# Two-layer hybrid encoder on eight cores: weights in runs of 512 columns, and another order of loads, transposes and stores

## The chip, the cores and the metric

One Trainium2 chip. The kernel runs on its 8 cores; each core takes one of the 8 sequences of the batch and holds nothing of the others. The time is the device time in microseconds of the slowest core, the median of several runs. A core has five engines that run side by side, each in the order of its own instructions: TensorE (PE) for matmuls, VectorE (DVE), ScalarE (ACT), GpSimd (POOL) and SyncE (SP). DMAs are issued by SP, ACT and POOL and run on 16 DMA engines per core.

## The reference

Two layers over x of 4096 positions by 1024 channels per core, then a final norm.

```python
def even_mixer(h, w_in, conv_w, conv_b, ln_g, ln_b, pool_w, pool_scale, w_out):
    z = h @ w_in                                                    # (B, S, 1536)
    a, gate, p = z[..., :D_A], z[..., D_A:2 * D_A], z[..., 2 * D_A:]
    ya = conformer_conv(a, gate, conv_w, conv_b, ln_g, ln_b)
    yb = multiscale_pool(p, pool_w, pool_scale)
    return jnp.concatenate([ya, yb], axis=-1) @ w_out

def spatial_gating(u, v, v_ln_g, v_ln_b, spatial_w, spatial_b):
    vn = layernorm(v.reshape(bn, s, N_SGU, H_D), v_ln_g, v_ln_b)
    vn = vn.reshape(bn, s // CHUNK, CHUNK, N_SGU, H_D)
    sv = jnp.einsum('hqk,bnkhc->bnqhc', spatial_w, vn) + spatial_b.T[:, :, None]
    return u * sv.reshape(bn, s, D_D)

for l in range(DEPTH):
    h = rmsnorm(x, mix_norm_g[l])
    x = x + (even_mixer if l % 2 == 0 else odd_mixer)(h, ...)
    h = rmsnorm(x, ffn_norm_g[l])
    x = x + (silu(h @ w_gate) * (h @ w_up)) @ w_down
return rmsnorm(x, final_norm_g)
```

`conformer_conv` is a gated linear unit, a depthwise convolution of width 31, a LayerNorm over 512 channels and a silu. `multiscale_pool` averages over centred windows of 2, 4, 8 and 16 positions. `odd_mixer` projects h to c (512 channels, a 2-D Fourier transform per head), and to u and v (a gelu, then the spatial gating above in chunks of 128 positions). The FFN is 2816 wide.

## The kernel before

The 4096 positions are 32 tiles of 128. A transposed, normalised activation of all tiles lives in `BIG` (32 tiles of 8 x 128 columns, 2 bytes each); matmuls read it as weights or as moving data, 512 columns at a time. Everything is written by hand in program order: `k.op`, `k.mm` and `k.dma` (L155 to L190) put the waits in front of each instruction, and every matmul has line L171, every DMA line L185, so one tells them apart by tiles. Weights are float32 in memory and become bfloat16 on the way; only POOL issues such DMAs (queue q0 in the profile). SP issues nearly all others (q1), transposes among them. `banks` hands out six PSUM banks in turn (eight in the odd layer's mixer).

Stages, in the order of the program:

1. *Even projections.* `norm_step` (L739) moves a tile through load (`n_load`), square and root (`n_stat`), scale, and transpose (`n_tr`: on TensorE for tiles 0 to 7, by DMA from SP after that). `p_proj` (L661) makes the pooling part and stores it through `pst`; `ag` (L670) makes gate and value and the gated unit. The list `jobs` mixes them, eight `p_proj` first. `n_load` of tiles from 2 on waits for the first third of the weights (`w_in`, `load_w_in`). `late_consts` loads the constants for the convolution after `ag` 3.
2. *Pooling and convolution*, `pool_bank` and `conv`, into `z`.
3. *First output projection, even layer.* `prologue` (L879) projects tiles 0 to 7: residual add on VectorE, norm, and a DMA transpose of `hbp`. Between its steps `feed0` (L904) runs the convolution's LayerNorm by groups of tiles: `ln_stat` (VectorE, POOL), `ln_norm` (ScalarE, into a ring of four tiles `vn`, then a DMA transpose into `BIG`), `ln_silu` (ScalarE, in place).
4. *FFN.* `ffn` (L476) goes over four chunks of 8 tiles: 22 steps j of gate and up (`up`: 32 matmuls of 512 columns, a ScalarE silu into `tmp`, a VectorE product), then eight tiles of the down projection. `Weights.fetch` keeps four steps of `wgu` in flight, 0.5 MB each as bfloat16, in every chunk anew; `wd` comes in the first chunk and stays. A table `steps` hangs the output projection of the next chunk's tiles (`op.load`, `op.mm`, `op.add`, `scale`, `tr`) on the steps j. In the first chunk `bg0` (L934) hangs the rest of the LayerNorm there too: for each group (n, a), `ln_stat` at j = a, `ln_norm` at a + 1, `ln_silu` at a + 2.
5. *Odd mixer.* `c_proj` (L987) for 16 tiles, its results through four staging tiles `cst` to memory; constants; then a loop over i with `u_proj`, `v_proj`, `v_stat`, `v_rs`, `v_norm` (four ScalarE operations a tile, one on POOL) and `sv` (L1067), staggered by up to 8 tiles, with the first Fourier steps (`f_first`) in between. Its last eight rounds have no projection left: each runs one `sv`, one `f_gcs_part`, one `f_s1` and one `v_norm`.
6. *Rest of the Fourier transform, prologue and FFN of the odd layer*, the same code as 3 and 4 without the LayerNorm, and the final norm.

`sv` adds the bias inside the matmul: for each of four heads a product with 128 rows, and one with 2 rows that carries the bias:

```python
mms.append((ps[:, b, h * 128:(h + 1) * 128], vn[:, t % 3, h * 128:(h + 1) * 128], swT[:, h, :], True, False))
mms.append((ps[:, b, h * 128:(h + 1) * 128], blT[0:2, h * 128:(h + 1) * 128],
            sbrow[0:2, h * 128:(h + 1) * 128], False, True))
```

## Time and profile before

| | |
|---|---|
| median of 3 runs | 2738.52 us (2737.62 to 2747.39) |
| profiled execution, own time | 2747.14 us |
| its span, slowest core (core 3) | 2746.0 us |
| spans of the 8 cores | 2727.0 to 2746.0 us |
| TensorE busy | 2584.3 us, 94% of the span, 12795 matmuls |
| VectorE, ScalarE, POOL busy | 812.7, 657.7, 331.6 us |
| chain that ended last | TensorE 84%, DMA 5%, SP's queue 4%, ScalarE 2%, issue 2% |
| DMA | 339.8 MB landed, HBM read 331.89 MB and written 83.89 MB |

A busy TensorE is one with matmuls in its pipeline; what counts beside it is the granted clock (1.00 is 2.4 GHz, 0.50 is 1.2 GHz) and the number of matmuls in a stretch. A wait is put down to the instruction that came last; idle time of an engine other than the one that sets the pace costs nothing by itself.

### The profile page before, as it was taken

What the parts mean: (1) busy time and instruction counts of PE and PEld (TensorE: products, weight loads), DVE (VectorE), ACT (ScalarE), POOL (GpSimd) and SP (SyncE); (2) the same over time, 40 slices, a digit from 0 to 9 for tenths busy, and PEclk for the clock granted to TensorE, in tenths of its full rate; (3) what the DMA queues carried; (4) which work ended last, traced back from release to release, by engine and by line L of the source; (5) the groups of instructions that cost most, each with busy time, mean ns of one, the idle gap of its engine ahead of it and who ended that gap; (6) DMA issues with size and microseconds to landing.
All of it is one profiled execution on the core that took longest, in us unless ns stands there. A gap on an engine that the chain in (4) does not pass through costs nothing.

```text
span 2746.0 us, 38570 instructions; the slowest of 8 cores (2727.0 to 2746.0 us)
## 1 busy us (share of the span) xinstructions
PE 2584.3 (94%) x12795; PEld 1210.6 (44%) x12795; DVE 812.7 (30%) x1175; ACT 657.7 (24%) x1163; POOL 331.6 (12%) x644
## 2 busy tenths in 40 slices
PE   5899786699999999999998998999999999999998
PEld 2346332344444444444443446444444444444443
DVE  2334532222222222222222445422222222222212
ACT  2333532311111121111113565211111111111111
POOL 1210111110100011000010341111011001100000
PEclk7999898899999999999999998999999999999999
DMA  6886689963665489444463104988356536554422
GB/s 150 189 174 141 154 134 127 131 144 125 126 126 137 126 158 154 139 102 77 111 152 92 70 9 98 205 165 169 93 123 132 115 108 127 124 119 108 77 45 95
DMA packets 257790, 339.80 MB, mean 124 GB/s; under 512 B 172350, under 2 KB 185152, under 8 KB 256448
## 3 DMA queue, kind: packets, MB, share of 16 engines
q1 hardware_dynamic: 222080, 218.68, 30.4%
q0 software_dynamic: 35376, 118.38, 26.5%
q8 instruction: 112, 1.84, 0.3%
q14 instruction: 78, 0.64, 0.1%
q10 hardware_dynamic: 144, 0.26, 0.0%
HBM read 331.89 MB, written 83.89 MB: 151 GB/s over the span
## 4 chain that ended last, share of the span: by engine, by line
PE 84%; DMA 5%; SPq 4%; ACT 2%; issue 2%; DVE 1%; POOL 1%; ACTq 0%; DVEq 0%; POOLq 0%
PE ps L171 84%; SPq L185 4%; DMA BIG_43<-vn_3454 2%; DMA xin_51<-x 1%; ACT BIG_43 L833 1%; DMA w_in_56<-ev_w_in 1%; ACT vt_12677 L1060 0%; DVE hb_91 L384 0%; POOL vn_12679 L1064 0%; DMA wd_3963<-ffn_wd 0%; DMA cdr<-cst_12665 0%; POOL rs_12682 L1046 0%; ACT vn_3454 L824 0%; ACT hb_91 L378 0%; DVE bst_2166 L804 0%
## 5 line engine op out<-in xcount | busy, mean ns | idle before, releaser
L171 PE MATMUL ps<-BIG_43,wgu_3455 128*128 128x512 bf16 x2816 | 621.4, 382 | 56.9 <-ACT tmp_3965 L495 43.6
L171 PE MATMUL ps<-BIG_43,wgu_16581 128*128 128x512 bf16 x2816 | 612.4, 379 | 0.0
L171 PEld LDWEIGHTS ps<-BIG_43,wgu_3455 128*128 128x128 bf16 x2816 | 276.8, 98 | 397.1 <-issue 71.1
L171 PEld LDWEIGHTS ps<-BIG_43,wgu_16581 128*128 128x128 bf16 x2816 | 275.6, 98 | 332.2
L171 PE MATMUL ps<-wd_3963,gT_3964 128*128 128x512 bf16 x1408 | 306.4, 380 | 3.8 <-DMA wd_3963<-ffn_wd 3.8
L171 PE MATMUL ps<-wd_16931,gT_16932 128*128 128x512 bf16 x1408 | 304.7, 379 | 2.6 <-DMA wd_16931<-ffn_wd 2.6
L497 DVE TENSOR_TENSOR gT_3964<-tmp_3965,ps 128x512 bf16<-128x512 f32 x176 | 120.9, 687 | 470.8 <-PE ps L171 361.8
L497 DVE TENSOR_TENSOR gT_16932<-tmp_16933,ps 128x512 bf16<-128x512 f32 x176 | 121.1, 688 | 419.6 <-PE ps L171 408.7
L171 PEld LDWEIGHTS ps<-wd_3963,gT_3964 128*128 128x128 bf16 x1408 | 138.2, 98 | 171.4 <-issue 6.5
L171 PEld LDWEIGHTS ps<-wd_16931,gT_16932 128*128 128x128 bf16 x1408 | 137.7, 98 | 168.9 <-issue 3.1
L495 ACT ACTIVATE tmp_16933<-ps 128x512 f32<-128x512 f32 x176 | 104.6, 594 | 395.4 <-PE ps L171 383.1
L495 ACT ACTIVATE tmp_3965<-ps 128x512 f32<-128x512 f32 x176 | 104.4, 593 | 365.6 <-PE ps L171 333.0
L171 PE MATMUL ps<-w_in_56,BIG_43 128*128 128x512 bf16 x768 | 178.5, 397 | 12.3 <-ACT sg_100 L679 7.9
L378 ACT ACTIVATE hb_3457<-xr_3456 128x1024 bf16<-128x1024 f32 x56 | 59.2, 1056 | 433.0 <-DVE xr_3456 L520 287.5
L361 POOL TENSOR_TENSOR ssb_44<-ssb_44,epsd_49 128x1 f32<-128x1 f32 x159 | 29.8, 188 | 1093.1 <-ACT hb_3457 L378 453.2
L171 PE MATMUL ps<-w_out_2713,BIG_43 128*128 128x512 bf16 x512 | 118.8, 387 | 16.7 <-ACT BIG_43 L833 16.3
L171 PEld LDWEIGHTS ps<-w_in_56,BIG_43 128*128 128x128 bf16 x768 | 77.6, 102 | 111.2 <-issue 28.6
L171 PE MATMUL ps<-w_in_12096,BIG_43 128*128 128x512 bf16 x512 | 115.5, 379 | 4.5 <-DVE cst_12665 L411 3.8
L171 PE MATMUL ps<-w_out_15705,BIG_43 128*128 128x512 bf16 x512 | 114.6, 379 | 1.1 <-ACT BIG_43 L409 1.1
L185 POOL DMA_DIRECT2D wgu_16581<-ffn_wgu x88 | 48.0, 546 | 482.5 <-PE ps L171 440.9
L185 POOL DMA_DIRECT2D wgu_3455<-ffn_wgu x88 | 48.5, 552 | 450.0 <-PE ps L171 449.6
L529 ACT ACTIVATE hb_16583<-xr_16582 128x1024 bf16<-128x1024 f32 x31 | 32.8, 1057 | 276.3 <-DVE xr_16582 L520 276.3
(150 smaller groups left out, 1749.5 us busy)
## 6 DMA issues: line engine op xcount, KB each, us to landing
wgu_3455<-ffn_wgu POOLq DMA_DIRECT2D x88, 512.0 KB, 6.0
wgu_16581<-ffn_wgu POOLq DMA_DIRECT2D x88, 512.0 KB, 5.4
xin_51<-x SPq DMA_DIRECT2D x32, 512.0 KB, 4.7
xr_3456<-xres SPq DMA_DIRECT2D x32, 512.0 KB, 3.9
xnat<-xr_3456 SPq DMA_DIRECT2D x32, 512.0 KB, 3.0
xr_16582<-xr SPq DMA_DIRECT2D x32, 512.0 KB, 5.5
out<-xr_16582 SPq DMA_DIRECT2D x31, 512.0 KB, 3.6
xr_3456<-x SPq DMA_DIRECT2D x28, 512.0 KB, 5.7
```

What stands on the lines that cost most here:

```text
L171: ins = self.nc.tensor.matmul(o, lhsT=l, rhs=r, start=st, stop=sp)
L185: ins = q.e.dma_start(out=o, in_=i, transpose=True) if transpose else q.e.dma_start(out=o, in_=i)
L361: k.op(pool, lambda e: e.tensor_tensor(out=ss, in0=ss, in1=epsd[:], op=ALU.add), reads=[d, d_epsd], writes=[d])
L378: k.op(act, lambda e: e.activation(out=h, in_=ap, func=AF.Square, accum_out=ssb[:, s, :]), reads=[dep], writes=[d_h, d_ss[s]])
L495: k.op(act, lambda e: e.activation(out=tmp[:], in_=ps[:, bl[0], :], func=AF.Silu), reads=[psd[bl[0]]], writes=[d_tmp])
L497: k.op(dve, lambda e: e.tensor_tensor(out=gT[:, j, tg * 512:(tg + 1) * 512], in0=tmp[:], in1=ps[:, bl[1], :], op=ALU.mult), reads=[d_tmp, ...
L529: k.op(act, lambda e: e.activation(out=h, in_=x, func=AF.Square, accum_out=ssb[:, s, :]), reads=[d], writes=[d_h, d_ss[s]])
L833: k.op(act, lambda e: e.activation(out=BIG[:, t0:t1, c, :], in_=BIG[:, t0:t1, c, :], func=AF.Silu, scale=evec[:, 0, c:c + 1], bias=evec[:, ...
```

## The change

It does nine things.

- All large weights and constants lie in memory as blocks of 128 rows by 512 columns, so that each row of a DMA is several runs of 512 elements (2 KB read, 1 KB landed) instead of one of 1024 to 4096. `dma_runs` and the layout in the host code.
- Start: x tiles 1 to 7 are issued at once, tiles 4 to 7 into a buffer of their own (`xin2`); the constants of the convolution come in three parts (after `ag` 5, 9 and 12).
- Stores of the pooling and of the c projection (`pst`, `cst`) go to ScalarE's queue; the c evacuations are all on ScalarE.
- The pooling tiles are loaded four to a DMA.
- LayerNorm groups are smaller at first; groups 0 to 4 (tiles 0 to 9) are transposed on TensorE, and the silu reads PSUM. The others keep the DMA transpose; their silu comes at j = a + 5 with new a's.
- FFN steps: the residual load two steps before its tile's base step, the projection one step after it; in the first chunk the tiles are two steps apart.
- The gating bias is one matmul of 8 rows by 512 columns, made with a selector (`sel8`, `sb8`), ahead of the four of 128 columns; `vn` has six tiles.
- The odd layer's constants are loaded during `c_proj` and used at i = 4 (`od_setup`); the Fourier constants (`gcs`) are loaded at i = 12 and 14.
- The gating loop ends with its 32nd round; the last tiles follow in a tail of their own, with the root per tile (`v_rs1`).

```diff
+        def dma_runs(q, o, i, **kw):
+            return k.dma(q, [(o.rearrange("p (b n) -> p b n", n=512), i.rearrange("b p n -> p b n"))], **kw)
...
-                    k.dma(pool, [(self.w[:, s], T["ffn_wgu"][self.l, self.n % NJ])], writes=[self.d[s]])
+                    dma_runs(pool, self.w[:, s].rearrange("p a b c -> p (a b c)"), T["ffn_wgu"][self.l, self.n % NJ],
+                             writes=[self.d[s]])
...
-                        s = (5 * n) // 2
+                        s = 3 + 2 * n if c == 0 else 1 + (5 * n) // 2
                         t = 8 * (c + 1) + n
-                        for q, fn in enumerate((op.load, op.mm, op.add, op.nrm.scale, op.nrm.tr)):
-                            steps.setdefault(s + (0, 1, 1, 2, 2)[q], []).append((fn, t))
+                        for pr, (j, fn) in enumerate(((s + 2, op.nrm.scale), (s + 2, op.nrm.tr), (max(0, s - 2), op.load),
+                                                      (s + 1, op.mm), (s + 1, op.add))):
+                            steps.setdefault(j, []).append((pr, n, fn, t))
...
-        k.dma(sp, [(xin[:, 1, :], T["x"][1])], writes=[d_xin[1]])
+        for t in range(1, 8):
+            n_load(t)
...
-            k.dma(sp, [(by_phase(pdr)[t // 16, t % 16], pst[:, r, :])], reads=[d_pst[r]], addw=[d_pdr[t // 16]],
+            k.dma(act, [(by_phase(pdr)[t // 16, t % 16], pst[:, r, :])], reads=[d_pst[r]], addw=[d_pdr[t // 16]],
...
-        groups = [(0, 2), (2, 4), (4, 8), (8, 12), (12, 16), (16, 20), (20, 24), (24, 28), (28, 32)]
+        groups = [(0, 2), (2, 4), (4, 6), (6, 8), (8, 10), (10, 13), (13, 16), (16, 20), (20, 24), (24, 28), (28, 32)]
...
         def ln_silu(n):
             t0, t1 = groups[n]
+            if n < LN_PE:
+                b = k.banks(2)
+                for t in range(t0, t1):
+                    v, d_v = lnv[t]
+                    k.mm([(ps[:, b + t - t0, c * 128:(c + 1) * 128], v[:, c * 128:(c + 1) * 128], ident[:], True, True)
+                          for c in range(4)], reads=[d_v, d_ident], writes=[psd[b + t - t0]])
+                for c in range(4):
+                    k.op(act, lambda e: e.activation(out=BIG[:, t0:t1, c, :], in_=ps[:, b:b + 2, c * 128:(c + 1) * 128],
...
-            for n, a in ((4, 1), (5, 3), (6, 6), (7, 9), (8, 12)):
+            for n, a in ((5, 0), (6, 2), (7, 4), (8, 7), (9, 10), (10, 13)):
                 if j == a:
                     ln_stat(n)
                 if j == a + 1:
                     ln_norm(n)
-                if j == a + 2:
+                if j == a + 5:
                     ln_silu(n)
...
-            evac(t % 2, cst[:, t % 4, :], ps[:, b, :], [psd[b]], [d_cst[t % 4]])
-            k.dma(sp, [(cdr[t * 128:(t + 1) * 128, :], cst[:, t % 4, :])], reads=[d_cst[t % 4]], addw=[d_cdr],
+            evac(0, cst[:, t % 4, :], ps[:, b, :], [psd[b]], [d_cst[t % 4]])
+            k.dma(act, [(cdr[t * 128:(t + 1) * 128, :], cst[:, t % 4, :])], reads=[d_cst[t % 4]], addw=[d_cdr],
...
-            mms = []
+            mms = [(ps[:, b, :], blT[0:8, :], sbrow[0:8, :], True, False)]
             for h in range(4):
-                mms.append((ps[:, b, h * 128:(h + 1) * 128], vn[:, t % 3, h * 128:(h + 1) * 128], swT[:, h, :], True,
-                            False))
-                mms.append((ps[:, b, h * 128:(h + 1) * 128], blT[0:2, h * 128:(h + 1) * 128],
-                            sbrow[0:2, h * 128:(h + 1) * 128], False, True))
+                mms.append((ps[:, b, h * 128:(h + 1) * 128], vn[:, t % 6, h * 128:(h + 1) * 128], swT[:, h, :], False,
+                            h == 3))
...
-        for i in range(NT + 8):
+        for i in range(NT):
...
+        v_stat(NT - 1)
+        v_rs1(NT - 1)
+        v_norm(NT - 6)
+        for n in range(4):
+            sv(NT - 8 + n)
+            v_norm(NT - 5 + n)
+            f_gcs_part(0, 4 * n)
+        v_norm(NT - 1)
+        for n in range(4):
+            f_gcs_part(0, 16 + 4 * n)
+            f_s1(1, range(8 * n, 8 * n + 8, 4))
+        for n in range(4):
+            sv(NT - 4 + n)
```

How the order of instructions moves, at three places. First SP, from the start of the program; `xin` and `xin_7` are x tiles, `hb` a normalised tile, `pdr` the pooling store. Before:

```order
L185 DMA xin_51<-x 128x1024
L185 DMA gbc_61<-norm_g 128x1024
L185 DMA xin_51<-x 128x1024 x2
L185 DMA pdr<-pst_99 128x512
L185 DMA xin_51<-x 128x1024
```

Now:

```order
L185 DMA xin_51<-x 128x1024
L185 DMA gbc_62<-norm_g 128x1024
L185 DMA xin_51<-x 128x1024 x3
L185 DMA xin_7_52<-x 128x1024 x4
L185 DMA xin_51<-x 128x1024 x2
L185 DMA_TRANSPOSE BIG_43<-hb_98 128x8x128
```

Ten x tiles stand ahead of the first transpose, and no store between them. Next ScalarE in the first steps of the even layer's first FFN chunk; `tmp` is the FFN silu, `vn` the LayerNorm's normalised tile, `BIG<-BIG,evec` its silu after a DMA transpose, `hb` the square of a norm. Before:

```order
L495 ACTIVATE tmp_3965<-ps 128x512
L824 ACTIVATE vn_3454<-z_29_2711,rs_2168 128x512 x4
L495 ACTIVATE tmp_3965<-ps 128x512 x2
L378 ACTIVATE hb_3457,ssb_44<-xr_3456 128x1024
L833 ACTIVATE BIG_43<-BIG_43,evec_46 128x4x128 x4
```

Now:

```order
L508 ACTIVATE tmp_3893<-ps 128x512 x5
L842 ACTIVATE vn_3355<-z_30_2633,rs_2114 128x512 x3
L508 ACTIVATE tmp_3893<-ps 128x512 x3
L842 ACTIVATE vn_3355<-z_30_2633,rs_2114 128x512 x3
L508 ACTIVATE tmp_3893<-ps 128x512 x2
L387 ACTIVATE hb_3358,ssb_44<-xr_3357 128x1024
L508 ACTIVATE tmp_3893<-ps 128x512 x2
L868 ACTIVATE BIG_43<-BIG_43,evec_46 128x3x128 x4
```

Seven FFN silus stand between the first group's normalisation and its silu, where two did. Last TensorE at the end of the gating, `gcs` and `f32m` being Fourier steps and `sbrow` the bias. Before, one of the last eight rounds:

```order
L171 MATMUL ps<-sbrow_12674,blT_12675 128x128
L171 MATMUL ps<-gcs_12667,Y_13664 128x128 x8
L171 MATMUL ps<-f32m_12673,ctm_12666 128x128 x4
L171 MATMUL ps<-swT_12670,vn_12679 128x128
L171 MATMUL ps<-sbrow_12674,blT_12675 128x128
```

Now:

```order
L171 MATMUL ps<-sbrow_12610,blT_12611 128x512
L171 MATMUL ps<-swT_12606,vn_12617 128x128 x4
L171 MATMUL ps<-gcs_12603,Y_13565 128x128 x16
L171 MATMUL ps<-f32m_12609,ctm_12602 128x128 x8
L171 MATMUL ps<-gcs_12603,Y_13565 128x128 x8
```

The Fourier steps stand together, ahead of the last four gating products.

## Rows read from the trace of the kernel before

**Rows 1.** Windows by stage: length; PE, PEld, DVE, ACT, POOL busy; PEclk, DMA share, GB/s

```profile
0.00:114.50 114.50, 75.14 (x323) 33.30 (x324) 31.19 (x29) 35.35 (x61) 20.14 (x54) 0.80 0.74 169
295.00:360.00 65.00, 42.80 (x178) 17.89 (x177) 30.88 (x48) 32.14 (x49) 12.28 (x28) 0.86 0.81 186
360.00:591.00 231.00, 179.55 (x794) 78.74 (x793) 61.62 (x103) 62.86 (x97) 36.36 (x70) 0.89 0.90 134
591.00:1410.00 819.00, 815.16 (x3770) 369.16 (x3769) 207.01 (x227) 130.67 (x226) 70.36 (x159) 1.00 0.55 125
1410.00:1451.00 41.00, 29.26 (x136) 12.60 (x134) 7.09 (x10) 5.21 (x9) 5.02 (x10) 0.96 0.94 184
1566.00:1626.00 60.00, 59.66 (x335) 31.27 (x336) 28.30 (x111) 38.09 (x76) 18.77 (x14) 1.00 0.00 1
1626.00:1668.60 42.60, 31.52 (x192) 18.79 (x193) 19.79 (x53) 23.15 (x47) 20.94 (x18) 0.61 0.21 59
1709.00:1919.00 210.00, 210.00 (x975) 95.19 (x973) 69.39 (x77) 45.03 (x77) 36.47 (x78) 1.00 0.88 179
```

**Rows 2.** Waits of TensorE, 295 to 592 us: total, times, longest

```profile
PE ps L171 <- ACT tmp_3965 L495: 43.6, 5, 20.5
PE ps L171 <- ACT BIG_43 L833: 16.3, 2, 9.1
PE ps L171 <- DVE xr_3456 L471: 7.7, 1, 7.7
```

**Rows 3.** Waits of ScalarE, 295 to 592 us

```profile
ACT BIG_43 L833 <- DMA BIG_43<-vn_3454: 66.8, 7, 23.2
```

**Rows 4.** DMA queues, 520 to 527 us: packets, MB, share of 16 engines

```profile
q0 software_dynamic: 401, 1.11, 85.4%
q1 hardware_dynamic: 509, 0.13, 27.6%
```

**Rows 5.** Chain that ended last, from the start: start us, us, what

```profile
1.65 14.18 DMA w_in_56<-ev_w_in
15.91 13.35 DMA xin_51<-x
```

**Rows 6.** Timeline of SP, 0 to 125 us: start us, us, what

```profile
40.03 0.33 SPq L185 DMA_DIRECT2D pdr<-pst_99  x1
40.51 0.33 SPq L185 DMA_DIRECT2D xin_51<-x  x1
```

**Rows 7.** Timeline of TensorE, 0 to 125 us

```profile
35.59 3.57 PE L171 MATMUL ps<-w_in_56,BIG_43 128*128 128x512 bf16 x8 [1.37 <-ACT BIG_43 L409]
...
44.94 0.61 PE L171 MATMUL ps<-ident_52,hb_91 128*128 128x128 bf16 x8
```

**Rows 8.** Groups of instructions, 284 to 345 us: busy us, mean ns; idle before

```profile
L833 ACT ACTIVATE BIG_43<-BIG_43,evec_46 128x256 bf16<-128x256 bf16 x8 | 4.8, 598 | 0.6
```

**Rows 9.** The page's DMA queues, whole run

```profile
q1 hardware_dynamic: 222080, 218.68, 30.4%
q0 software_dynamic: 35376, 118.38, 26.5%
```

**Rows 10.** DMA queues, 1415.6 to 1418 us, small constants

```profile
q0 software_dynamic: 263, 0.24, 83.3%
```

**Rows 11.** Timeline of POOL, 1385 to 1470 us

```profile
1415.30 0.56 POOL L185 DMA_DIRECT2D f32m_12673<-f32m  x1
```

**Rows 12.** Timeline of SP, 1410 to 1452 us

```profile
1422.06 10.59 SPq L185 DMA_TRANSPOSE BIG_43<-hdr  x1
```

**Rows 13.** Timeline of TensorE, 1574 to 1592 us: one tile's gating product, then Fourier

```profile
1576.20 0.22 PE L171 MATMUL ps<-swT_12670,vn_12679 128*128 128x128 bf16 x1
...
1577.47 0.62 PE L171 MATMUL ps<-f32m_12673,ctm_12666 128*128 128x128 bf16 x8
1577.93 1.89 PE L171 MATMUL ps<-w_in_12096,BIG_43 128*128 128x512 bf16 x8
```

**Rows 14.** Timeline of all engines, 1626 to 1669 us

```profile
1632.09 2.25 ACT L1060 ACTIVATE vt_12677<-vt_12677,rs_12682 128x128 f32<-128x128 f32 x4 [3.01 <-DVE rs_12682 L1052]
```

More of the change, by code:

```diff
@@ L221, with runs @@
 NAT = 16 * (np.arange(128) % 8) + np.arange(128) // 8
+def runs(a, n=512):
+    a = np.asarray(a).reshape(128, -1, n)
+    return np.ascontiguousarray(a.transpose(1, 0, 2))
 def make_consts():
@@ L242, in make_consts @@
     band = band[:, :, :, NAT]
-    c["band"] = np.ascontiguousarray(band.transpose(2, 0, 1, 3)).astype(np.float32)
+    c["band"] = runs(band.transpose(2, 0, 1, 3).astype(np.float32))
     c["ident"] = np.eye(128, dtype=np.float32)
@@ L586, in ffn @@
                     W.fetch(c * NJ + j + 1 + NSLOT)
-                    for fn, t in steps.get(j, []):
+                    for _, _, fn, t in sorted(steps.get(j, []), key=lambda x: x[:2]):
                         fn(t)
                     if c == 0:
-                        k.dma(pool, [(wd[:, j, :], T["ffn_wd"][l, j])], writes=[d_wd[j]])
+                        dma_runs(pool, wd[:, j, :], T["ffn_wd"][l, j], writes=[d_wd[j]])
                     if bg is not None:
@@ L722, in p_load @@
                 pbuf[t] = (t_[:, t - lo], d_[t - lo])
-                k.dma(sp, [(t_[:, t - lo], pdr[t])], reads=[d_pdr[t // 16]], writes=[d_[t - lo]])
+            for t in range(lo, hi, 4):
+                n = min(4, hi - t)
+                k.dma(sp, [(t_[:, t - lo:t - lo + n], pdr[t:t + n].rearrange("t p d -> p t d"))],
+                      reads=[d_pdr[t // 16], d_pdr[(t + n - 1) // 16]], writes=d_[t - lo:t - lo + n])
         jobs = [(p_proj, t) for t in range(8)]
@@ L809, in ln_stat @@
             m = t1 - t0
[L810 to L813 removed]
+            rstd(rs[:, r, 0, 0:m], mv[:, r, 0:m, 1], False, [d_mv[r]], d_rs[r])
         def ln_norm(n):
@@ L827, in ln_norm @@
                      reads=[d_z[t // 16][t % 16], d_mv[r], d_rs[r]], writes=[d_v])
-                k.dma(sp, [(BIG[:, t, 0:4, :], v)], reads=[d_v], writes=[dB[t][0]], transpose=True)
+                if n >= LN_PE:
+                    k.dma(sp, [(BIG[:, t, 0:4, :], v)], reads=[d_v], writes=[dB[t][0]], transpose=True)
+                else:
+                    lnv[t] = (v, d_v)
+        lnv = {}
+        LN_PE = 5
         def ln_silu(n):
             t0, t1 = groups[n]
+            if n < LN_PE:
[6 more added lines that the diff above has]
+                    k.op(act, lambda e: e.activation(out=BIG[:, t0:t1, c, :], in_=ps[:, b:b + 2, c * 128:(c + 1) * 128],
+                                                     func=AF.Silu, scale=evec[:, 0, c:c + 1], bias=evec[:, 1, c:c + 1]),
+                         reads=[d_evec, psd[b], psd[b + 1]], addw=[dB[t][0] for t in range(t0, t1)])
+                return
             for c in range(4):
@@ L905, in feed0 @@
             if i == -2:
-                ln_stat(0)
-                ln_norm(0)
-                ln_stat(1)
-                ln_norm(1)
+                for n in range(2):
+                    ln_stat(n)
+                    ln_norm(n)
+            if i == -1:
                 ln_silu(0)
-                ln_stat(2)
-                ln_norm(2)
-                ln_silu(1)
             if i == 0:
                 Wf.fetch(NSLOT)
-            if i == 1:
-                ln_silu(2)
-            if i == 5:
-                ln_stat(3)
-            if i == 6:
-                ln_norm(3)
-            if i == 8:
-                ln_silu(3)
-        prologue(op, 3, 2, feed0)
+            if i in (1, 3, 5):
+                ln_silu(1 + i // 2)
+                if i < 5:
+                    ln_stat(2 + i // 2)
+                    ln_norm(2 + i // 2)
+            if i == 7:
+                ln_stat(4)
+                ln_norm(4)
+            if i == 9:
+                ln_silu(4)
+        prologue(op, 2, 2, feed0)
         nrm2 = Norm(None, hbr)
@@ L1249, in prep_inputs @@
     g["od_vln"] = _rep(f(inputs["od_v_ln_g"])[0].reshape(512))
-    g["od_vln_b"] = np.stack([f(inputs["od_v_ln_b"])[0].reshape(512), np.ones(512, np.float32)])
+    vb = f(inputs["od_v_ln_b"])[0].reshape(4, 128)
+    g["od_vln_b"] = np.stack([vb, np.ones_like(vb)], axis=1).reshape(8, 128)
     sw = f(inputs["od_spatial_w"])[0]
     g["od_spatial_wT"] = np.ascontiguousarray(sw.transpose(2, 0, 1))
-    g["od_spatial_b"] = np.ascontiguousarray(f(inputs["od_spatial_b"])[0]).reshape(1, 512)
+    sb = np.zeros((4, 2, 4, 128), np.float32)
+    for h in range(4):
+        sb[h, 1, h] = f(inputs["od_spatial_b"])[0][h]
+    g["od_spatial_b"] = sb.reshape(8, 512)
     g.update(make_consts())
```

216 lines of the change are left out of this document (118 added, 98 removed).

## The prediction

> **What bounds the kernel now.** I read the stretches by stage first [rows 1]. In the long FFN stretch TensorE is busy for 815 of 819 us at full granted clock: 3770 matmuls, 0.216 us each. The reader is to look for stretches where that pace is lost. There are four. The first 114.5 us (busy 75, clock 0.80). The even layer's first output projections with the first FFN chunk, 65 + 231 us for 178 + 794 matmuls: the odd layer runs the same loop, 975 matmuls, in 210 us without a gap. The start of the odd layer (29.3 of 41). The end of the spatial gating, 42.6 us at clock 0.61. Then the waits say who ends them. Between 295 and 592 us TensorE waits 43.6 us for the FFN's ScalarE silu, 16.3 us for the LayerNorm silu and 7.7 us for a residual tile [rows 2]; but ScalarE itself waits 66.8 us, in seven pieces, for DMA transposes of the LayerNorm tiles [rows 3]. ScalarE works in order, so the FFN silu stands behind a LayerNorm silu whose tile hasn't landed. The DMA rows tell why: in seven microseconds 509 small packets of q1 (the transposes) went by 401 large ones of q0 (weights) [rows 4], about one for one, so each transpose packet sits out a weight packet.
>
> So the bound is TensorE, plus some 160 us (2746 less 2584 busy) in which it stands still. The change goes at these places; whole matmul time is nearly untouched.
>
> **The change, part by part.** A measurement of this kernel can tell about 0.5% (14 us) from no change.
>
> *Start.* Now the first weights land at 15.8 us, and x tile 2, which waits for them, at 29.3 [rows 5]; later tiles are loaded behind the store of a projection in SP's order [rows 6], so every tile pays one projection, one load and one norm in a row. At 114.5 us TensorE has done 233 of its 512-column matmuls (323 less 26 for warming and 64 transposes), 50 us at 0.216, and 64 transposes (eight in 0.61 us [rows 7], 5 us): it is 60 us behind. The change issues x 1 to 7 at once, into buffers that are free, and moves the stores to ScalarE's queue. By 29.3 us the chip had read 3 x 2.1 MB of weights, 0.5 MB of norm scale and three x tiles of 0.52 MB, 8.4 MB; the new start needs 11 MB before the last weights are there, at the same pace 38 us. Weights and x share that pace, so I put the first weights at 21 us instead of 15.8. Eight projections, each with a transpose, then cost between 2.3 us (8 x 0.216 + 0.61) and 4.2 us (3.57 + 0.61, at the clock of that stretch [rows 7]) each; I take 3.5, nearer the slow end, since TensorE has just stood idle, 28 us, to 49 us, with 14 + 5 us of that useful: 30 behind. ScalarE still meets the load of tile 12 ahead of the first sigmoid; 6 us for it. 36 instead of 60: **gain 24**, between 12 (all cold, loads as late as now) and 36.
>
> *LayerNorm of the even layer.* Tiles 0 to 9 go through TensorE: 5 pairs of 8 transposes at 0.61 us add 3 us. The silu reads PSUM in pairs: four at 0.60 us [rows 8], so three times in the prologue TensorE waits some 2.7 us, 8 us; the first chain stays at about 5, the last transposed tile of the prologue at 4, clock lost around these 3. Tiles 10 to 31 keep the DMA but the silu comes four FFN steps after the transpose instead of one, some 30 us instead of 8, and no wait for one took longer than 23.2 us [rows 3]. What is late next is the ring of four normalised tiles: ScalarE must wait for a slot before the next group; 5 us for that. Of the 86 us over the odd layer's 210, 28 stay: **gain 58**, between 30 (half of the silu waits come back through the ring) and 72. Loads of the residual three steps ahead are in it (7.7 us).
>
> *Weights in runs of 512.* A fetch of 0.52 MB becomes 512 packets of 1 KB instead of 128 of 4 KB. Price by the rows, in microseconds of one of 16 engines per MB landed: q0 over the whole run 0.265 x 16 x 2746 / 118.4 = 98 [rows 9]; a moment with small constants, 1 KB packets mostly, among other traffic 0.833 x 16 x 2.4 / 0.24 = 133 [rows 10]. I take 115, in between, since the second row is a crowded moment. The dearest place is the first FFN chunk, 22 x (0.52 + 0.26) MB = 17.3 MB: 124 us of each engine, beside 13.4 MB of other traffic (8 tiles read, written and transposed, 22 LayerNorm tiles) at q1's 61 (0.304 x 16 x 2746 / 218.7), 51 us. 175 us against the 185 us that TensorE needs: covered, narrowly. At 133 it would be 195, and 10 us in each layer show; at 98 nothing does. Cost 0; the range takes 20. The longer descriptor lists are written by POOL; nothing in the trace shows such a list. Below: no dearer than now, 0.56 us for 128 rows [rows 11]. Above: in proportion, 4.5 us for each of three weight loads ahead of tile 0's norm, 13 us, of which the weights' own landing hides most. I take 1 us each, on no path.
>
> *Odd layer's start.* TensorE is idle 41 - 29.3 = 11.7 us there [rows 1]: the four staging tiles of the c projection wait for stores that stand in SP's order behind transposes, one of which took 10.6 us to issue [rows 12]. Stores move to ScalarE's queue, with all evacuations; ScalarE is busy 5 of these 41 us and has room. **Gain 10**, between 6 and 12; constants and their 24 copies move under the u and v projections. The Trainium skill (DMA: Bandwidth & Descriptors, Issuing engines are not separate DMA queues) says that issuing from several engines saves only the issue time. By that the 16 stores would give SP some 8 us and TensorE nothing; the 10.6 us issue ahead of a store speaks for the gain, a matter of order and not of bandwidth.
>
> *Gating bias.* Eight 128-column matmuls of a tile, 128 rows and 2 rows by turns, take 1.27 us from the first's start to the end of the turns, 0.16 each, while eight like ones in a row give way after 0.46, 0.06 each [rows 13]. One of 512 columns (0.22), four at 0.06 and two changes at 0.1 make 0.65 instead of 1.27: 0.62 on each of 24 tiles where TensorE is full (59.7 of 60 us), **gain 14**, between 3 (only the number of instructions counts) and 19.
>
> *Gating tail.* The new tail has no rounds that wait one for the other. ScalarE bounds it: six normalisations at 2.25 us [rows 14], 13.5, some evacuations, 2.4, and 3 us to the last product, after 4 us of v projection: 23 instead of 42.6. **Gain 20**, between 12 and 32.
>
> The rest I put at 0: pooling tiles loaded in groups of four and the FFN steps of the later chunks lie where TensorE runs through.
>
> Sum: 24 + 58 + 10 + 14 + 20 = **126 us**. The profiled run took 2747.1, so 2621; it stands 8.6 above the median, 2738.5, and against that the forecast is **2612**.
>
> **The rivals.** *Weight packets still go out in bundles.* The Trainium skill (DMA: Bandwidth & Descriptors, Queues, rings and completion order) says that a DMA engine drains a packet of many descriptors from one ring before it turns to the next. By that rule four runs of 1 KB would pass as one 4 KB did. Worked from the rows: transposes are then as slow as now [rows 4], the ring of four tiles fills and most of the silu waits come back, in the first chunk and at the prologue's last tile: the 58 falls below its low end, to some 25. Gain 126 - 33 = 93, time 2645. For it: no row has small weight packets beside transposes. Against it: 1.27 transpose packets per weight packet, so turns are short. 0.14.
>
> *The start stays bound by reading.* x and weights share the chip's memory; if eight cores at once get less than 0.29 MB per us, x and weights land at 45 us and the gain there is about 6: 2630. 0.10. The DMA share of 0.74 [rows 1] leaves either open.
>
> *Weights come too late (slower).* In both first chunks, if 1 KB runs cost far more than 133. At 200 per MB the weights alone take 216 us of each engine, with the rest 267 against 185: 82 us lost in each layer; the other six chunks, 11.5 MB and 40 us of other traffic against 177, lose 7 each. 206 - 126 = 80 slower: 2819. It begins at 124, where the first chunks just fit (134 + 51 = 185), and turns the sign near 183 (198 + 51 - 185 = 64, twice). No row here is above 133 [rows 10]: 0.03.
>
> **How the numbers follow.** My forecast has 0.73, with 2575 to 2650 from the bounds of the terms (all low ends together 63, 2675; all high ones 171, 2567; they won't all fall on one side). The two fast rivals lie at 2645 and 2630. The range, **2575 to 2680**, leaves out the slow rival and the far ends. Faster by over 0.5% 0.96, within 0.5% 0.01, slower 0.03: even the low ends of all terms are 2.3%.
>
> **What would show it.** Right: the same waits between the prologue and the end of the first chunk add up to under 30 us, ScalarE's wait for LayerNorm transposes to under 10; that whole stretch takes some 238 us; TensorE is in its stride by 60 us; the gating tail takes about 25 us at a higher clock; q0's share rises from 26.5% to about 31%. Wrong: TensorE waits for weights in the first chunks, ScalarE waits for slots of the LayerNorm ring, or transposes still take 20 us beside weights.

## The result, and the profile after

The changed kernel takes 2674.92 us (median of 4 runs, 2664.44 to 2678.49); the kernel before, beside it, 2742.95 (4 runs). The ratio is 0.9744, interval 0.9705 to 0.9784: 68 us faster, where 126 were forecast. The profiled execution took 2678.49 us.

Spans of three cores in that execution, with the mean granted clock:

```profile
core 2: 2660.5 us, clock 0.983
core 3: 2657.3 us, clock 0.983
core 6: 2676.4 us, clock 0.979
```

Seven cores lie between 2657 and 2662; core 6 ends 15 us later and gives the time. Before, core 3 was the slowest; in the other three runs of the changed kernel cores 2, 4 and 4 were. Rows below are of core 2, a middle one, unless another is named.

The table shows by stage where the time went. Each number is the median over the 8 cores of one profiled execution, in us, between two events of the trace. The first two columns count from the start: to the first sigmoid, and to the first pooling product, where the input projections end. Then: first output projection to first FFN silu (prologue); from there to the 44th silu (chunk 1); to the 45th (its down projection); first staging tile of the c projection to VectorE's first product of u with the gate (odd start); to the last gelu of v (gating); to the first norm of the next prologue (tail). Where an edit leaves a stage alone, its entries spread over at most 4 us, in the last four columns over 2.

```
                  sigmoid  proj.end  prologue  chunk 1   down  odd start  gating   tail
before               80.6     232.5      58.8    214.2   86.2      108.2   116.2   79.6
changed              81.6     231.2      58.9    176.5   87.6       91.3   111.5   65.8
long rows            77.5     228.4      58.9    193.7   85.7       91.3   112.3   65.7
silu near            81.0     232.8      58.0    208.2   87.2       91.3   112.3   65.5
DMA transposes       81.4     232.5      67.1    174.8   87.5       90.5   113.3   66.3
early x              73.1     218.0      59.0    177.6   88.8       91.3   112.3   65.5
early x, long w_in   68.3     213.3      59.0    178.8   87.6       91.3   111.5   65.5
SP stores            78.3     226.9      59.9    176.5   87.3       91.3   111.5   66.0
table early          80.4     229.7      60.2    176.5   87.2       91.3   112.3   65.5
table early, SP st.  78.0     227.1      58.4    176.7   88.0      102.3   113.1   65.5
constants early      81.1     229.4      58.9    176.5   87.3       91.3   111.5   66.0
bias by turns        81.8     232.2      58.8    176.6   87.6       91.8   117.6   71.6
old tail             81.2     231.0      59.6    176.5   87.2       91.3   109.8   75.2
combined             69.3     213.9      49.7    178.0   81.2       91.3   111.5   65.8
```

From before to changed, chunk 1 gave 38, the odd start 17, the tail 14, gating 5, the start 1, the prologue nothing, and the down projection took 1. The sum is 73; between the two slowest cores it is 70, since core 6 stood further above the middle than core 3 had.

Windows by stage, columns as in [rows 1], of the start, the prologue and chunk 1:

```profile
0.00:60.00 60.00, 27.25 (x136) 12.47 (x137) 15.36 (x14) 19.43 (x31) 10.37 (x29) 0.77 0.74 163
293.00:352.00 59.00, 38.81 (x180) 16.99 (x178) 28.11 (x42) 28.03 (x49) 13.36 (x30) 0.87 0.74 165
352.00:529.00 177.00, 177.00 (x818) 80.11 (x817) 64.70 (x110) 67.43 (x105) 44.46 (x70) 1.00 1.15 173
```

Chunk 1 runs through at full clock now. In the start and the prologue TensorE is still idle for half and a third of the time. Its waits in the prologue, 290 to 352 us (total, times, longest):

```profile
PE ps L171 <- ACT BIG_43 L863: 7.9, 2, 5.5
PE ps L171 <- ACT vn_3355 L842: 5.0, 3, 3.4
PE ps L171 <- DVE xp_2656 L484: 4.2, 1, 4.2
PE ps L171 <- DVE hbp_3359 L393: 2.4, 1, 2.4
```

Its waits from 0 to 145 us, where norms, weights and one sigmoid hold it up:

```profile
PE ps L171 <- DVE hb_98 L393: 19.0, 5, 4.8
PE ps L171 <- DMA w_in_58<-ev_w_in: 11.8, 1, 11.8
PE ps L171 <- ACT sg_107 L699: 6.9, 2, 6.3
```

The answer to [rows 2, 3]: TensorE's waits for the FFN silu, 43.6 us on core 3, are gone from chunk 1. Of ScalarE's 66.8 us for transposes this is left in its waits from 348 to 592 us, a wait for a slot of the ring of four:

```profile
ACT vn_3355 L842 <- DMA BIG_43<-vn_3355: 6.5, 2, 4.8
```

The page's groups, which are of core 6, name what that core lost: 6.6 us for a residual tile, for which no other core waits in chunk 1, and 8.4 us for down weights, for which the others wait 3.9 to 5.8. That is some 10 of its 15 us.

```profile
L171 PE MATMUL ps<-BIG_43,wgu_3356 128*128 128x512 bf16 x2816 | 616.6, 381 | 7.0 <-DVE xr_3357 L484 6.6
...
L171 PE MATMUL ps<-wd_3891,gT_3892 128*128 128x512 bf16 x1376 | 305.3, 382 | 10.1 <-DMA wd_3891<-ffn_wd 8.4
```

The page's queues, against [rows 9]:

```profile
q0 software_dynamic: 120016, 118.40, 30.9%
q1 hardware_dynamic: 206768, 208.71, 29.3%
```

The same weights in 3.4 times as many packets cost 0.309 x 16 x 2676 / 118.4 = 112 us of an engine per MB, where 98 was the price before and 115 was assumed.

### The profile page after: what moved, and what is told of

It is laid out like the page before. It is cut to its first block, busy times and chain, and to the rows that moved or that the text cites. A ratio compares the mean times of both kernels' runs of the same rounds, so it can differ in the third digit from the quotient of the medians.

```text
span 2676.4 us, 38177 instructions; the slowest of 8 cores (2657.3 to 2676.4 us)
## 1 busy us (share of the span) xinstructions
PE 2545.3 (95%) x12585; PEld 1193.9 (45%) x12739; DVE 802.3 (30%) x1166; ACT 665.8 (25%) x1186; POOL 385.2 (14%) x655
## 4 chain that ended last, share of the span: by engine, by line
PE 86%; DMA 3%; SPq 3%; issue 2%; POOL 2%; DVE 2%; ACT 2%; another core or an unknown queue 1%; ACTq 0%; DVEq 0%; POOLq 0%
PE ps L171 86%; SPq L185 2%; DMA xin_51<-x 2%; ACT vt_12615 L1114 1%; DMA xr_3357<-x 1%; DVE hb_98 L393 1%; POOL vn_12617 L1118 0%; DMA wd_3891<-ffn_wd 0%; POOL rs_12620 L1091 0%; DMA wd_16768<-ffn_wd 0%; ACT hb_98 L387 0%; DMA gbc_62<-norm_g 0%; POOL ssb_44 L373 0%; DVE bst_2112 L825 0%
## 5 line engine op out<-in xcount | busy, mean ns | idle before, releaser
L171 PE MATMUL ps<-BIG_43,wgu_3356 128*128 128x512 bf16 x2816 | 616.6, 381 | 7.0 <-DVE xr_3357 L484 6.6
L171 PE MATMUL ps<-BIG_43,wgu_16418 128*128 128x512 bf16 x2816 | 612.4, 379 | 0.0
L171 PE MATMUL ps<-wd_3891,gT_3892 128*128 128x512 bf16 x1376 | 305.3, 382 | 10.1 <-DMA wd_3891<-ffn_wd 8.4
L171 PE MATMUL ps<-wd_16768,gT_16769 128*128 128x512 bf16 x1376 | 305.3, 382 | 6.5 <-DMA wd_16768<-ffn_wd 4.8
L171 PE MATMUL ps<-w_in_58,BIG_43 128*128 128x512 bf16 x751 | 174.7, 392 | 24.2 <-DMA w_in_58<-ev_w_in 12.2
L185 POOL DMA_DIRECT2D wgu_16418<-ffn_wgu x88 | 66.9, 760 | 470.0 <-PE ps L171 456.0
L171 PE MATMUL ps<-w_out_2635,BIG_43 128*128 128x512 bf16 x485 | 112.1, 385 | 16.0 <-ACT BIG_43 L863 8.3
L185 POOL DMA_DIRECT2D wgu_3356<-ffn_wgu x88 | 67.3, 766 | 413.9 <-PE ps L171 400.1
L171 PE MATMUL ps<-w_in_12032,BIG_43 128*128 128x512 bf16 x495 | 112.6, 379 | 2.4 <-DVE xr_3357 L533 1.5
L171 PE MATMUL ps<-w_out_15542,BIG_43 128*128 128x512 bf16 x485 | 109.1, 379 | 2.7 <-ACT BIG_43 L422 1.4
```

The source lines that it names most:

```text
L171: ins = self.nc.tensor.matmul(o, lhsT=l, rhs=r, start=st, stop=sp)
L185: ins = q.e.dma_start(out=o, in_=i, transpose=True) if transpose else q.e.dma_start(out=o, in_=i)
```

## The experiments

Twelve kernels ran. Each is the changed one with one part undone or moved; three carry two or more edits, as named. Ratios are to the kernel before. Their intervals reach some 10 us to either side, so the smaller verdicts go by the stages of the table.

### First chunk: distance, packets, transposes

**Long rows.** All weights again as one row per partition; the other shapes follow the two shown.

```diff
-    return k.dma(q, [(o.rearrange("p (b n) -> p b n", n=512), i.rearrange("b p n -> p b n"))], **kw)
+    return k.dma(q, [(o, i)], **kw)
-    "ffn_wgu": [2, NJ, 4, 128, 512],
-    "ffn_wd": [2, NJ, 2, 128, 512],
+    "ffn_wgu": [2, NJ, 128, 2048],
+    "ffn_wd": [2, NJ, 128, D],
```

> The change with the weights' long rows put back (one descriptor per partition and tile, as before), all else kept. Theory A (the silu's distance and the transposes on TensorE brought the gain of the first FFN chunk, the length of the runs does little for it): the first chunk, from the first FFN silu to the 45th, stays within 6 us of the 177 that the middle core takes with the change, and the time within 8 us of 2675. Theory B (short packets let the transposes by, and that brought the gain): the chunk is 20 us or more longer, 2690 to 2710. Theory C (short runs cost: they are behind the waits of up to 8 us for the down weights): those waits halve, the share of q0 goes from 31% back to about 27%, and the time is 5 to 12 us shorter.

Ratio 0.9784 (0.9735 to 0.9832), profiled 2697.38 us. Chunk 1 took 193.7 us, 17 more, from 186 to 216 by core: between A's 6 and B's 20, nearer B. The rows on the tile vn from 352 to 560 us say how long a LayerNorm transpose took to land. Of the changed kernel:

```profile
DMA to landing us min/median/max: 9.5/13.6/17.8
```

The same with long rows:

```profile
DMA to landing us min/median/max: 4.9/17.6/33.1
```

By core the slowest took 22 to 33 us with long rows and 15 to 20 with short ones. The distance from a normalisation to its silu is four steps (4 x 177 / 22 = 32 us). Only core 2's slowest, with long rows, is longer, and on no core does a silu wait for a landing. What comes late is the next normalisation: the ring of four is full, and ScalarE waits for a slot, 348 to 592 us, on core 2:

```profile
ACT vn L841 <- DMA BIG<-vn: 33.7, 9, 7.2
```

TensorE, in the same stretch, then waits for the FFN silu behind it:

```profile
PE ps L171 <- ACT tmp L507: 21.6, 2, 18.9
```

Theory C fell, though short runs do cost at another place: with long rows the first projection began at 19.3 us instead of 29.9.

**Silu near.** The silu of the first chunk one step behind its normalisation.

```diff
-                if j == a + 5:
+                if j == a + 2:
                     ln_silu(n)
```

> The change with the LayerNorm silu of the first FFN chunk back at one step behind its normalisation instead of four; transposes on TensorE and short runs kept. Theory A (the distance made the gain): ScalarE waits again 20 to 50 us for DMA transposes, the first chunk takes 195 to 210 us instead of 177, time 2690 to 2710. Theory B (short packets make a transpose land in time anyway): ScalarE waits under 10 us, chunk within 5 us of 177, time within 8 us of 2675.

Ratio 0.9810 (0.9749 to 0.9872), chunk 1 208.2 us, 32 more: theory A. ScalarE's wait on the core where it was longest, core 6, 348 to 592 us:

```profile
ACT BIG L868 <- DMA BIG<-vn: 51.4, 5, 16.7
```

So the distance is worth 32 us with short runs in place, the runs 17 with the distance in place, and both together with the rest 38: each covers a part of what the other does. The finer groups, their new steps and the earlier residual loads were not undone by themselves.

**DMA transposes.** No LayerNorm tile turned on TensorE.

```diff
-        LN_PE = 5
+        LN_PE = 0
```

> The change with the LayerNorm tiles 0 to 9 transposed by DMA too, the finer groups and the distance of four steps in the first chunk kept. Theory A (the transposes on TensorE serve the prologue): the prologue, 58 us with the change, takes 64 to 80, since the silu there follows its normalisation by at most one projection pair and waits for the landing, 7 us at the median and up to 15; the first chunk stays at 177. Theory B (the prologue's time is set by the chain of sums, norms and silu, and not by how the tile is turned): 58 to 61 us, since it took 59 before, with DMA transposes.

Ratio 0.9758 (0.9708 to 0.9808), prologue 67.1 us, 8 more: theory A, near its low end. TensorE's waits for the silu, 290 to 352 us:

```profile
PE ps L171 <- ACT BIG L868: 21.6, 4, 13.9
```

The transposes on TensorE save 8 us against that, and yet the prologue is no faster than before: the new order puts each pair's transposes and silu right in front of the projection that needs them, and takes the 8 us back. The run *Combined* below shows it: with the order moved, the prologue takes 49.7 us.

### The start

**Early x.** Loads six and three steps earlier, into the same buffers.

```diff
-            if 8 <= i < NT:
-                n_load(i)
+            if 2 <= i < 6:
+                n_load(i + 6)
+            if 9 <= i < NT - 3:
+                n_load(i + 3)
```

> The change with tiles 8 to 11 of x asked for six steps ahead and later ones three steps ahead of where they stood in SP's order, into the same buffers. Theory A (loads from tile 10 on stand behind transposes in SP's order, and ScalarE meets their norms ahead of the first sigmoid): the first sigmoid comes at 62 to 70 us instead of 82, the projections end 10 to 18 us earlier than at 231, time 2657 to 2666. Theory B (the start is bound by reading): the first sigmoid stays within 3 us of 82, and so does the end of the projections; time within 5 us of 2675.

Ratio 0.9660 (0.9615 to 0.9704). The first sigmoid came at 73.1 us instead of 81.6, the end of the projections at 218.0 instead of 231.2: theory A by the end, though the sigmoid moved less than it said. The reason stands in the changed kernel. SP's timeline there on core 6 (start us, us):

```profile
11.63 5.82 SPq L185 DMA_DIRECT2D xin_51<-x  x2
63.03 1.34 SPq L185 DMA_TRANSPOSE BIG_43<-hb_98  x1
64.54 0.45 SPq L185 DMA_DIRECT2D xin_51<-x  x1
```

ScalarE's timeline, same core, with the waits ahead in brackets:

```profile
69.98 1.06 ACT L387 ACTIVATE hb_98<-xin_51 128x1024 bf16<-128x1024 f32 x1 [10.10 <-DMA xin_51<-x]
...
80.70 1.06 ACT L387 ACTIVATE hb_98<-xin_51 128x1024 bf16<-128x1024 f32 x1 [6.63 <-DMA xin_51<-x]
...
81.75 0.58 ACT L699 ACTIVATE sg_107<-ps 128x512 f32<-128x512 f32 x1
```

SP issues nothing from 17.5 to 63 us: the load of tile 10, whose buffer tile 2 left long ago, stands behind the first DMA transpose, which waits for the norm of tile 8. ScalarE then waits 10.1 and 6.6 us for loads, ahead of the sigmoid that TensorE waits for.

**Early x, long w_in.** The same, and the even layer's input weights in long rows.

```diff
-    "ev_w_in": [3, 8, 128, 512], "od_w_in": [3, 8, 128, 512],
+    "ev_w_in": [3, 128, 8, 512], "od_w_in": [3, 8, 128, 512],
```

> The run with the earlier x loads, and the even layer's three input weights alone put back to one long row per partition (8 KB in SBUF), all other weights in runs of 512. With all weights in long rows the first projection began at 19 us instead of 30. Theory A (the short runs make the first weights late by 10 us, and with the loads out of the way this delay is on the path): first projection at 18 to 21, first sigmoid at 64 to 69 instead of 73, projections end at 207 to 213 instead of 218, time 5 to 11 us under the run with early loads, 2649 to 2656. Theory B (norms and transposes of the first tiles set the pace, not the weights): the first projection moves by 10, the first sigmoid by under 4, the time by under 4.

Ratio 0.9663 (0.9632 to 0.9695). First projection at 19.2 us, 11 earlier, sigmoid at 68.3, end of the projections 4.7 earlier: between the theories. TensorE's waits for norms from 0 to 145 us grew from 17.7 us (core 2, with early x alone) to

```profile
PE ps L171 <- DVE hb L393: 25.0, 6, 7.3
```

so 7 of the 11 us come back there. Why the weights were late is told by the DMA queues from 8 to 20 us (packets, MB, share of 16 engines). The changed kernel:

```profile
q1 hardware_dynamic: 657, 2.38, 64.7%
q0 software_dynamic: 646, 0.62, 41.6%
```

The kernel with all rows long:

```profile
q0 software_dynamic: 232, 1.51, 77.0%
q1 hardware_dynamic: 233, 0.84, 26.8%
```

The two queues' packets are one for one, 657 to 646 and 233 to 232, whatever their size. For each weight packet of 1 KB a packet of x of 3.6 KB goes by, and the weights get a fifth of the bytes landed; with packets of 6.5 KB they get two thirds.

### The odd layer's start

**SP stores.** The stores of both projections back on SP.

```diff
-            k.dma(act, [(by_phase(pdr)[t // 16, t % 16], pst[:, r, :])], reads=[d_pst[r]], addw=[d_pdr[t // 16]],
+            k.dma(sp, [(by_phase(pdr)[t // 16, t % 16], pst[:, r, :])], reads=[d_pst[r]], addw=[d_pdr[t // 16]],
...
-            k.dma(act, [(cdr[t * 128:(t + 1) * 128, :], cst[:, t % 4, :])], reads=[d_cst[t % 4]], addw=[d_cdr],
+            k.dma(sp, [(cdr[t * 128:(t + 1) * 128, :], cst[:, t % 4, :])], reads=[d_cst[t % 4]], addw=[d_cdr],
```

> The change with the stores of the pooling projection and of the c projection back on SP's queue, all else kept (all evacuations of the c projection stay on ScalarE). Theory A (SP's order held the odd layer's start, and the stores brought the 17 to 20 us that it gained): from the first store tile of the c projection to the first u tile, 29 us with the change, it takes 38 to 48 again, and the start of the even layer 3 to 8 more; time 2688 to 2700. Theory B (the constants, their copies and matmuls, moved under the u and v projections, brought it): 29 to 33 us, time 2675 to 2680.

Ratio 0.9714 (0.9663 to 0.9766). Theory A fell: the odd start stays at 91.3 us, and the even layer's start is 4 us faster, not slower. The stretch named in the expectation was badly chosen. It took 35.2 us for 29, which is only a later gelu on ScalarE; TensorE's longest wait there is 1.5 us, and up to the first gating product it lost nothing.

**Table early**, and **table early with SP stores**. The second has the edit above too.

```diff
-            if i in (12, 14):
-                dma_runs(pool, gcs[:, (i - 12) // 2].rearrange("p a b -> p (a b)"), T["gcs"][(i - 12) // 2],
-                         **{"writes" if i == 12 else "addw": [d_gcs]})
...
+        for i in range(2):
+            dma_runs(pool, gcs[:, i].rearrange("p a b -> p (a b)"), T["gcs"][i],
+                     **{"writes" if i == 0 else "addw": [d_gcs]})
```

> The change with the load of the large Fourier table (4.2 MB read, 2.1 MB landed) back at the head of the odd layer, all else kept; stores stay on ScalarE's queue. With the stores alone back on SP nothing was lost, so the question is what had made SP's transposes slow there. Theory A (the table's load fills the DMA engines, transposes and stores then land late, and with stores off SP that still costs): the stretch from the first staging tile of the c projection to the first gating product, 91 us with the change, takes 97 to 108. Theory B (only both together cost, or neither): 91 to 93.

> The change with the table's load back at the head of the odd layer and the stores of both projections back on SP's queue. Theory A (before, stores stood behind transposes that the table's load had made slow; either cure alone suffices): the stretch of 91 us takes 100 to 108, as against 91 with the stores alone put back. Theory B (the 17 us came from elsewhere, the constants' matmuls and copies): 91 to 94.

Ratios 0.9719 (0.9692 to 0.9746) and 0.9754 (0.9719 to 0.9789); the stretch took 91.3 and 102.3 us. Neither alone costs, both together 11. With both, SP's timeline (core 2) shows a transpose that takes 9 us to issue, as [rows 12] did, and the next store behind it:

```profile
1366.61 9.13 SPq L185 DMA_TRANSPOSE BIG<-hdr  x1
1375.84 0.53 SPq L185 DMA_DIRECT2D cdr<-cst  x1
```

TensorE's waits, 1350 to 1470 us, name the staging tiles again:

```profile
PE ps L171 <- ACT cst L422: 5.7, 2, 3.4
```

**Constants early.** All small constants at tile 0, their matmuls and copies ahead of the first u projection.

```diff
-            if i == 4:
+            if i == 0:
                 od_setup()
```

> The change with the odd layer's small constants loaded at the head of the c projection and their matmuls and 24 ScalarE copies ahead of the first u projection again, the table late and the stores on ScalarE's queue. Theory A (the copies ahead of the u projections cost TensorE their time): the stretch of 91 us takes 95 to 100, TensorE waiting for the constants' products or for ScalarE. Theory B (ScalarE has room, TensorE goes on into free banks): 91 to 92.

Ratio 0.9732 (0.9677 to 0.9787), stretch 91.3 us: theory B. So 6 of this stage's 17 us are in none of these undoings; all of them together were not tried, nor were the evacuations shared with VectorE again, as before.

### Gating and tail

**Bias by turns.** Four bias matmuls of 128 columns, one behind each of the other four.

```diff
-            mms = [(ps[:, b, :], blT[0:8, :], sbrow[0:8, :], True, False)]
+            mms = []
...
+                mms.append((ps[:, b, h * 128:(h + 1) * 128], blT[0:8, :], sbrow[0:8, h * 128:(h + 1) * 128], False,
+                            True))
```

> The change with the gating bias again as four matmuls of 128 columns, by turns with the four of the gating itself (8 rows instead of 2), all else kept. Theory A (TensorE is no longer what sets the pace of the gating; the saved 0.62 us per tile came back as waits for the normalised tile): TensorE is busy 8 to 14 us longer between 1445 and 1560 us, its waits there fall by as much as 5 to 8, and the time grows by only 3 to 6 us, to 2678 to 2681. Theory B (TensorE sets the pace, and the gain was lost somewhere else): the stage from the first gating product to the last v projection grows by 12 to 15 us, time 2687 to 2690.

Ratio 0.9745 (0.9701 to 0.9789). Gating took 6 us longer, the tail 6. In the gating that is theory A, in the tail the full price and a little more (8 tiles at 0.62 are 5.0). The windows show it. By turns, from 1450 us:

```profile
1450.00:1568.00 118.00, 112.53 (x612) 56.82 (x622) 55.09 (x226) 73.13 (x146) 49.37 (x38) 0.99 0.18 41
```

The changed kernel, the same work:

```profile
1448.00:1560.00 112.00, 98.29 (x554) 46.74 (x551) 54.99 (x226) 73.09 (x148) 49.45 (x39) 0.99 0.22 48
```

TensorE is busy 14.2 us less, and the stretch is 6 us shorter; the other 8 are waits. One of them in TensorE's timeline of the changed kernel, core 6:

```profile
1508.49 0.37 PE L171 MATMUL ps<-sbrow_12610,blT_12611 8*128 8x512 bf16 x1 [1.69 <-POOL vn_12617 L1118]
```

What POOL did then, same core:

```profile
1503.89 2.92 POOL L1091 TENSOR_TENSOR rs_12620<-rs_12620,cst_3_45 128x16 f32<-128x16 f32 x1
1506.79 1.25 POOL L1118 TENSOR_TENSOR vn_12617<-vt_12615,vln_12605 128x512 bf16<-128x512 f32 x1
```

The power for four later tiles, 2.92 us, stands in POOL's order ahead of the tile that the next product needs.

**Old tail.** The rounds of before, with the statistics of the last four tiles in one group.

```diff
-        for i in range(NT):
+        for i in range(NT + 8):
...
+            if i >= NT:
+                f_gcs_part(0, 4 * (i - NT))
+                f_s1(1, range(4 * (i - NT), 4 * (i - NT) + 4, 4))
```

> The change with the gating's tail put back to the rounds of before (eight rounds that each take one product, one part of the Fourier mix and one of the first step, the normalisation two rounds ahead, one group of four statistics at the end), the bias as one matmul kept. Theory A (the new order of the tail brought what was forecast, 20 us): the stretch from the last v projection to the end of the Fourier mix, 66 us with the change, grows by 18 to 22, time 2693 to 2697. Theory B (the single bias matmul brought most of what was seen there and the order little; putting the bias back cost 4 us in the tail and 2.5 behind it): it grows by 5 to 9, time 2680 to 2684.

Its time is that of two runs, 2672.74 and 2680.32 us, too few for an interval. Gating and tail together took 7.7 us longer: theory B.

### Combined

Early x and long w_in, and two orders more.

```diff
-            if i in (1, 3, 5):
-                ln_silu(1 + i // 2)
+            if i == 1:
+                ln_silu(1)
...
+            if i in (2, 4, 6):
+                ln_silu(1 + i // 2)
...
+                    if c == 0:
+                        dma_runs(pool, wd[:, j, :], T["ffn_wd"][l, j], writes=[d_wd[j]])
                     W.fetch(c * NJ + j + 1 + NSLOT)
```

> Early x loads and long rows for the even layer's input weights, and two orders changed: in the prologue each pair's transposes and silu one projection ahead of their use instead of right before it, and in the first FFN chunk the down weights of a step asked for ahead of the next gate weights. Expected: the prologue (first output projection to first FFN silu, 58 us) 5 to 8 us shorter, since two waits of 2.4 and 2.6 us and some cold clock go; the down projection's waits for its weights at the end of the first chunk from 5 us to under 2; with the start together 15 to 25 us under the change, 2645 to 2658. If the down weights' waits stay, they wait for the engines and not for POOL's order.

Ratio 0.9585 (0.9553 to 0.9618), profiled 2639.84 us: faster than both kernels, the interval apart from the changed kernel's. The window of the prologue:

```profile
275.00:325.00 50.00, 37.05 (x180) 16.85 (x182) 26.83 (x41) 27.80 (x50) 12.63 (x29) 0.90 0.88 178
```

The same 180 matmuls as in 59 us, in 50, more than the 5 to 8 expected; with early x and long w_in alone it took 59.0, so the order made it. The down projection took 81.2 us, 6 less, and all stages together 31 us less than with the change, where 15 to 25 were expected. The wait for down weights is under 1.5 us on five cores; on three it is still 5 to 6, so POOL's order was not all of it.

## Why the prediction was right and wrong

Sign and range held, the size did not: 73 us on the middle core for the 126. That the range held is in part luck. The time, 2675, is that of all the terms' low ends together, of which the prediction said that they wouldn't all fall on one side; the start fell below its own low end, and the odd start went above its high one.

- *Start: forecast 24, measured 1.* Three steps failed. "Weights and x share that pace, so I put the first weights at 21 us": they share it by packets. In long rows the weights land in time for a projection at 19 us, in short ones at 30; that is a cost of the runs, which I had put at 0. And "ScalarE still meets the load of tile 12 ahead of the first sigmoid; 6 us for it": the loads from tile 10 on stand behind transposes and cost 10.1 + 6.6. These two put right gave 18 us. Third, the projections at 3.5 us each, 4.2 at most: on core 6 six of them took from 30.4 to 60.2 us, 5.0 each, since TensorE waits ahead of every second one for the next two norms:

```profile
40.05 0.61 PE L171 MATMUL ps<-ident_53,hb_98 128*128 128x128 bf16 x8 [3.28 <-DVE hb_98 L393]
...
59.42 1.01 PE L171 MATMUL ps<-ident_53,hb_98 128*128 128x128 bf16 x8 [3.91 <-DVE hb_98 L393]
```

  No run cured these waits. The rival of a start bound by reading comes near the gain there, with 6, but its mechanism fell. Counted as read (a weight byte landed is two read), core 2 had 10.4 MB by 36 us and 11.7 by 40, so the 11 MB came at some 38 us, as forecast, and asking for x earlier, at much the same pace, ended the projections 13 us sooner.
- *LayerNorm: forecast 58, measured 38.* "Of the 86 us over the odd layer's 210, 28 stay": on the middle core 25 stay (58.9 + 176.5 - 210), so the mechanism and the remainder were right. The base was not. The 86 come from core 3, whose chunk 1 took 234 us against the middle core's 214; core 3 did gain 58 there, but then another core was the slowest. In the prologue the three waits between a pair's transposes and its projection, priced at 8 as waits for the silu, are 4.2 + 2.4 + 2.4 = 9, two of them ended by a residual add and a norm, while the 3 for the clock were too few at 0.87 over 59 us. The ring of four was late next, as said.
- *Runs: forecast 0.* The price was right, 112 for 115. That they bring 17 us of chunk 1 and cost 10 at the first weights was not seen, although [rows 4] had shown the queues taking turns.
- *Odd start: forecast 10, measured 17.* A store behind a 10 us transpose was the right wait, but the late table cures it as well. The Trainium skill (DMA: Bandwidth & Descriptors, Issuing engines are not separate DMA queues) says that issuing from several engines saves the issue time only. With the table late the runs agree with it, 91.3 us from either queue. With the table early the other queue is worth 11 us (102.3 against 91.3): still issue time, but that of the transpose ahead of the store, 9.13 us.
- *Gating bias: forecast 14, measured 5 (6 by undoing it).* "0.62 on each of 24 tiles where TensorE is full" (24 x 0.62 is 14.9, not 14) is right in the first half: TensorE is busy 14.2 us less. Once it is not full, it waits for POOL and for the normalisation's scales: 10.4 us between 1448 and 1560 on core 2. Eight more products in the tail brought 6 that stood under no step.
- *Tail: forecast 20, measured 14,* of which 6 are the bias's and 8 the new order's. "ScalarE bounds it" left out the chain ahead of ScalarE. TensorE's waits, 1560 to 1583 us:

```profile
PE ps L171 <- ACT vt_12615 L1114: 6.3, 2, 5.7
PE ps L171 <- POOL rs_12620 L371: 4.8, 1, 4.8
```

  and the clock in that window is 0.59, not higher as I had said. From the last but one v projection to the last gating product, 42.6 us before, it took 34, not 23.
- *Bundles.* The rival fell: with short rows transposes do land sooner than with long ones, 15 to 20 us at worst instead of 22 to 33. They land no sooner than in the kernel before, whose worst were 17 to 21 by core while its silus held the next normalisation up; the gain over that kernel is that ScalarE no longer waits right behind them (*Silu near*). The Trainium skill (DMA: Bandwidth & Descriptors, Queues, rings and completion order) has an engine change queues after a packet of many descriptors; the trace agrees that the queues take turns, and its counts (657 to 646, 233 to 232) show that four short runs did not go by as one; how many packets make a turn they don't tell. *Weights too late* came in small only: 4 to 8 us for down weights at the end of chunk 1, where it was 3 to 6 before.

Of the marks named, these held: waits from the prologue to the end of chunk 1 under 30 us (19.5), ScalarE's under 10 (6.5), the stretch some 238 us (235), q0 at 31%. TensorE in stride by 60 us and a tail of 25 us at a faster clock did not. All three signs of being wrong came too, each in small: TensorE's waits for down weights, ScalarE's 6.5 us, which is a wait for a slot of the ring, and transposes of up to 19.5 us.

## What to carry to other kernels

Read a stage's loss on a middle core as well as on the slowest: what only the slowest lost, another core may lose next time. Where two DMA queues compete, the length of their rows divided the bytes between them here, so short rows suit what can wait and long ones what everybody waits for. And a load whose buffer is free does not belong behind a transpose in the same queue, nor a silu right in front of its use.

## What the hardware showed unasked

The queues' packets stayed one for one at quite different sizes, 3.6 KB beside 1 KB (657 to 646) and beside 6.5 KB (233 to 232). And stores moved from SP to ScalarE's queue made the even layer's start 4 us slower, not faster, in both runs that moved them back (226.9 and 227.1 against 231.2); why was not looked into.
